# A two-layer transformer block on one core: a written-out loop on the PE, reordered ACT and DVE pieces, and a third weight buffer

## The chip, the core and the metric

The kernel runs on one core of one Trainium2 chip. The metric is device time in microseconds (us), lower is better. The core has five engines that run their own instruction streams and meet only at semaphores: PE (TensorE, the matrix multiplier), DVE (VectorE), ACT (ScalarE), POOL (GpSimd) and SP, which here only issues DMAs.

## The reference

The program computes two layers (`DEPTH = 2`) over 512 latent tokens and 256 context tokens of width 1024, in fp32.

```python
for l in range(DEPTH):
    need_ctx = l < DEPTH - 1
    a_lat = modulate(x, norm1_g[l], mod_lat[0], mod_lat[1])      # rms_norm(x, g) * (1 + scale) + shift
    a_ctx = modulate(h, norm1_g[l], mod_ctx[0], mod_ctx[1])
    m_lat, m_ctx = token_mixers(a_lat, a_ctx, w_in[l], w_out[l], ...)   # attention | retention | Fourier
    x = x + mod_lat[2] * m_lat
    x = x + mod_lat[5] * sq_relu_mlp(modulate(x, norm2_g[l], mod_lat[3], mod_lat[4]), w_ff1[l], w_ff2[l])
    if need_ctx:
        h = h + mod_ctx[2] * m_ctx
        h = h + mod_ctx[5] * sq_relu_mlp(modulate(h, ...), w_ff1[l], w_ff2[l])
```

`sq_relu_mlp(h, w1, w2)` is `square(relu(h @ w1)) @ w2` with a hidden width of 4096. The retention part needs tables of decay factors, made with exp from `ret_decay_logit[l]`. Context tokens are carried through the first layer only; the second layer updates the latent tokens alone.

## The kernel before

**Layout.** The residual stream `X` stands transposed: 8 tiles (m = 0 to 7) of 128 features by 768 tokens, the 512 latent ones first. Every fp32 product is made of three matmuls with operands split in a high and a low part: high by high, high by low, low by high. So every weight tile goes through three hands: SP loads 128x1024 values to `raw` (`w_load`, line 339), ACT copies them to `Whi` (`hi`, line 658, one at line 663), POOL subtracts to get `Wlo` (`low_parts`, line 521). `raw`, `Whi` and `Wlo` have two slots; unit u of the weights uses slot u % 2, and a slot comes free when the PE has finished the unit two before. At the end of the first layer there is a third slot (`raw3`, which lies in `macc`, and `W3`), used in turn with the other two by 13 units (`in_tail`, `slot_of`, `slot_before`, `raw_count`, lines 280 to 298).

**Order.** Everything is ordered by hand: each engine's function (`_(sp)`, `_(pool)`, `_(act)`, `_(dve)`, `_(pe)`) lists its work in program order, and a wait at the head of an engine's stream holds all behind it. Loop variable l is 0 for the first layer and 1 for the second. Per layer: 18 units of the input projection (`for u in range(UP)`, five groups g of output columns), transposes, retention and attention, 8 units of the output projection, then the MLP: four tiles of the first weight matrix, seven `half(c, ...)` of four tiles of the first and four units of the second matrix each, and a rest.

**The PE's loops.** In the first layer `half(0)`, `half(1)` and `half(2)` are written out on the PE and `half(3)` to `half(6)` are a hardware loop of two passes of two halves (line 2056). In the second layer three passes of two halves are a loop (line 2099). In the first layer the halves also turn modulation sums (`mod_sums`, four transposes from `macc`, line 1577) after their fifth and eighth unit.

**The norms.** `NORMS` numbers six of them: 1 and 2 are the ones ahead of the first layer's MLP (latent, context), 3 and 4 those at the start of the second layer (latent, context), 5 the one ahead of the second layer's MLP. A norm n goes through these pieces: ACT squares each of the 8 tiles of `X` as soon as its residual is added (`stat_squares`, line 688, alternately to `sqb[:, 0]` and `sqb[:, 1]`), DVE adds the squares up to `sq_sums` (`sq_add`, line 1118), the PE sums over features with matmuls against ones (`stats`, line 1595: first `sq_sums`, which holds tiles 0 to 6, then tile 7), ACT takes the root (`norm_root`), DVE the reciprocal, the PE spreads it (`spread`), and then for every tile DVE multiplies (`norm_full`, line 1092), ACT makes the high part (`norm_hi`, line 706) and DVE (even tiles; all tiles in norms 3 and 4) or POOL (odd tiles) the low part.

**The second layer's start.** In the input projection's first group (units 0 to 3) four banks of PSUM fill; ACT copies them to `Pq` after unit 3 (line 814), and unit 4 overwrites them. Beside that ACT makes the decay tables: `prep` (line 722, after unit 1) and `prep_tables` (line 733, after unit 2), 17 instructions in all with three loads of function tables; DVE makes `prep_gains`, `prep_masks` and the squares of the queries (`q_squares`) by the list `work` (line 1289).

## Time and profile before

| | before |
|---|---|
| median of 3 runs | 1704.47 us (1702.3 to 1705.03) |
| the profiled execution | 1702.21 us |
| its span, first to last instruction | 1700.4 us |
| mean granted PE clock | 0.977 |
| PE busy | 1606.9 us, 94% |
| DVE busy | 1042.7 us, 61% |
| ACT busy | 588.5 us, 35% |
| POOL busy | 584.6 us, 34% |

The busy shares are averages over stages. The span is 1.8 us shorter than the execution's own time, which also holds what lies before the first and behind the last instruction. Positions in the text ("at 813.95") are us from the span's start. A matmul is listed with the length of its pipeline, so neighbours overlap; the distance between two starts is what one costs. Two records of the same kind may stand merged in one row, with their number behind x.

### The profile page before, as it was taken

How to read it: one execution, taken by the hardware profiler on the slowest of the kernel's cores; microseconds unless marked ns; L12 is line 12 of the kernel's file. 1: busy time of each engine (PE TensorE's matmuls, PEld its weight loads, DVE VectorE, ACT ScalarE, POOL GpSimd, SP SyncE). 2: the span in 40 equal slices, each digit the busy share in tenths (PEclk: the TensorE clock that was granted, in tenths of full speed). 3: DMA queues.
4: the chain of work that ended last, by engine and by line, in shares of the span. 5: the costliest groups of instructions: out<-in, count | busy, mean ns of one | idle time of the engine just before them, and what ended most of it. 6: DMA issues, size and time to landing. Idle time of an engine off the chain costs nothing.

```text
span 1700.4 us, 23038 instructions
## 1 busy us (share of the span) xinstructions
PE 1606.9 (94%) x8800; PEld 1365.0 (80%) x8800; DVE 1042.7 (61%) x1481; ACT 588.5 (35%) x951; POOL 584.6 (34%) x324
## 2 busy tenths in 40 slices
PE   6899989989999999999899988998999799999998
PEld 2788878978888888888788887887897688888887
DVE  5778966868765767566466776585544544444442
ACT  4522435652532221211212345234662432332321
POOL 1336661012333222233222443336003444444442
PEclk9899999989999999999999999999999899999999
DMA  9333111105333434344343432231002132333332
GB/s 325 101 126 118 51 44 50 51 9 154 94 99 116 120 112 131 99 142 133 91 143 103 129 110 75 71 91 38 1 1 82 55 99 88 97 95 90 99 99 87
DMA packets 168653, 162.33 MB, mean 95 GB/s; under 512 B 6624, under 2 KB 132208, under 8 KB 168560
## 3 DMA queue, kind: packets, MB, share of 16 engines
q1 hardware_dynamic: 168560, 161.02, 31.1%
q8 instruction: 67, 1.10, 0.3%
q14 instruction: 26, 0.21, 0.0%
HBM read 158.90 MB, written 2.10 MB: 95 GB/s over the span
## 4 chain that ended last, share of the span: by engine, by line
PE 57%; issue 25%; DVE 7%; POOL 4%; ACT 4%; DMA 1%; SPq 1%; POOLq 0%; DVEq 0%; ACTq 0%
PE psA L1931 17%; PE psB L1931 16%; POOL Wlo L525 4%; PE psA L1711 2%; PE psA L1712 2%; PE psA L1713 2%; PE psB L1711 2%; PE psB L1713 2%; PE psB L1712 2%; PE ps L1903 2%; DVE Ab L1438 1%; PE psS L1713 1%; PE psS L1712 1%; PE psS L1711 1%; PE psS L1572 1%
## 5 line engine op out<-in xcount | busy, mean ns | idle before, releaser
L525 POOL TENSOR_TENSOR Wlo<-raw,Whi 128x1024 fp32r<-128x1024 f32 x158 | 384.5, 2434 | 829.8 <-ACT Whi L663 829.8
L663 ACT ACTIVATE Whi<-raw 128x1024 fp32r<-128x1024 f32 x181 | 191.4, 1059 | 635.0 <-PE psB L1931 269.4
L1438 DVE TENSOR_TENSOR Ab<-Tb 128x512 f32<-128x512 f32 (+2 forms) x68 | 167.9, 2469 | 175.9 <-ACT Tb L929 175.8
L1931 PE MATMUL psA<-Ahi,Whi 128*128 128x512 f32 (+1 forms) x432 | 138.1, 362 | 11.4 <-issue 5.0
L1931 PE MATMUL psB<-Ahi,Whi 128*128 128x512 f32 (+1 forms) x424 | 135.1, 362 | 2.6 <-POOL Wlo L529 2.2
L1931 PE MATMUL psA<-Ahi,Wlo 128*128 128x512 f32 (+1 forms) x432 | 137.5, 361 | 0.0
L1931 PE MATMUL psA<-Alo,Whi 128*128 128x512 f32 (+1 forms) x432 | 136.8, 359 | 0.0
L1931 PE MATMUL psB<-Ahi,Wlo 128*128 128x512 f32 (+1 forms) x424 | 134.9, 361 | 0.0
L1211 DVE SCALAR_TENSOR_TENSOR X<-psB,modT,X 128x256 f32<-128x256 f32 (+1 forms) x104 | 67.1, 664 | 109.7 <-PE psB L1931 109.6
L1931 PE MATMUL psB<-Alo,Whi 128*128 128x512 f32 (+1 forms) x424 | 134.3, 359 | 0.0
L1931 PE MATMUL psA<-Hhi,Whi 128*128 128x512 f32 (+1 forms) x368 | 117.7, 362 | 14.1 <-DVE X L1211 12.8
L1211 DVE SCALAR_TENSOR_TENSOR X<-psA,modT,X 128x256 f32<-128x256 f32 (+1 forms) x104 | 67.0, 662 | 86.2 <-PE psA L1931 86.1
L1039 DVE SCALAR_TENSOR_TENSOR macc<-modraw,csil,macc 128x512 f32<-128x512 f32 x126 | 113.2, 957 | 10.4 <-DMA modraw<-in_w_mod_dram 10.4
L1931 PE MATMUL psA<-Hhi,Wlo 128*128 128x512 f32 (+1 forms) x368 | 116.6, 359 | 0.0
L1931 PE MATMUL psB<-Hhi,Wlo 128*128 128x512 f32 (+1 forms) x368 | 116.3, 358 | 0.0
L1931 PE MATMUL psA<-Hlo,Whi 128*128 128x512 f32 (+1 forms) x368 | 115.9, 357 | 0.0
L1931 PE MATMUL psB<-Hhi,Whi 128*128 128x512 f32 (+1 forms) x368 | 115.9, 357 | 0.0
L1931 PE MATMUL psB<-Hlo,Whi 128*128 128x512 f32 (+1 forms) x368 | 115.7, 357 | 0.0
L931 ACT ACTIVATE Hhi<-Ab 128x512 fp32r<-128x512 f32 (+2 forms) x68 | 48.2, 708 | 176.6 <-DVE Ab L1438 176.6
L1931 PEld LDWEIGHTS psA<-Ahi,Whi 128*128 128x128 f32 x432 | 74.5, 190 | 25.0 <-issue 7.9
L1931 PEld LDWEIGHTS psA<-Hhi,Whi 128*128 128x128 f32 x368 | 62.8, 189 | 29.0 <-issue 9.8
L1440 DVE TENSOR_TENSOR Hlo<-Ab,Hhi 128x512 fp32r<-128x512 f32 (+2 forms) x68 | 53.5, 786 | 52.7 <-ACT Hhi L931 52.7
(331 smaller groups left out, 3525.9 us busy)
## 6 DMA issues: line engine op xcount, KB each, us to landing
raw<-in_w_ff_dram SPq DMA_DIRECT2D x135, 512.0 KB, 4.1
modraw<-in_w_mod_dram SPq DMA_DIRECT2D x72, 512.0 KB, 4.3
raw<-in_w_in_dram SPq DMA_DIRECT2D x36, 512.0 KB, 3.7
modst<-in_w_mod_dram SPq DMA_DIRECT2D x16, 512.0 KB, 5.8
raw<-in_w_out_dram SPq DMA_DIRECT2D x16, 512.0 KB, 4.3
modat<-in_w_mod_dram SPq DMA_DIRECT2D x8, 512.0 KB, 3.8
macc<-in_w_ff_dram SPq DMA_DIRECT2D x5, 512.0 KB, 3.5
modraw<-in_dft_lat_dram SPq DMA_DIRECT2D x8, 257.0 KB, 3.6
```

The source lines that it names most:

```text
L525: nc.gpsimd.tensor_tensor(Wlo[:, s, :], raw[:, s, :], Whi[:, s, :], ALU.subtract).then_inc(S["lo_done"], 1)
L663: nc.scalar.activation(whis[slot], raws[slot], ACT.Copy).then_inc(S["hi_done"], 1)
L931: nc.scalar.activation(Hhi[:, hpar, k, c0:c1], Ab[:, k % 2, c0:c1], ACT.Copy).then_inc(S["h_hi"], 1)
L1039: ins = V.scalar_tensor_tensor(out=acc[:, s, :], in0=src[:, kk * MCH:(kk + 1) * MCH], scalar=col, in1=acc[:, s, :], op0=ALU.mult, op1=ALU.add)
L1211: last = V.scalar_tensor_tensor(out=X[:, m, c0:c1], in0=pair[p][:, c0:c1], scalar=modT[:, l, 8 * chunk + m, s:s + 1], in1=X[:, m, c0:c1], ...
L1438: V.tensor_tensor(Ab[:, k % 2, c0:c1], Tb[:, k % 2, c0:c1], Tb[:, k % 2, c0:c1], ALU.mult).then_inc(S["h_full"], 1)
L1440: V.tensor_tensor(Hlo[:, hpar, k, c0:c1], Ab[:, k % 2, c0:c1], Hhi[:, hpar, k, c0:c1], ALU.subtract).then_inc(S["h_lo"], 1)
L1711: mm(out, ah, wh, start=first, stop=False)
L1712: mm(out, ah, wl, start=False, stop=False)
L1713: last = mm(out, al, wh, start=False, stop=fin)
L1903: last = mm((ps6, ps7)[b % 2][:, h * HD:(h + 1) * HD], PTs[:, it % 2, i * P:(i + 1) * P], Pk[:, kt, P + (h // 4) * HD:P + (h // 4 + 1) * H ...
L1931: last = mm(dst[:, c0:c1], wt, x[:, i, c0:c1], start=f, stop=e)
```

## The change

- **The PE's loop in the first layer is written out.** `half(3)` to `half(6)` become four straight copies.
- **Token sums in three parts.** DVE adds only tiles 0 to 5 to `sq_sums`; the PE sums `sq_sums`, then tile 6 from `sqb[:, 0]`, then tile 7 from `sqb[:, 1]`. The last `sq_add` of each of the norms 1 to 5 goes, and each `stats` gets one more round of token-tile matmuls (4 for latent, 2 for context tokens).
- **Norm pieces behind residuals.** In norm 3 DVE and ACT take the context residuals 4 to 7 ahead of the last norm tiles: DVE's order becomes residuals 2, 3, tiles 3, 4, residuals 4, 5, tile 5, residuals 6, 7, tiles 6, 7. Before norm 1's root ACT no longer squares the first context tile.
- **Decay tables in units 4 and 5** (counted from 0) of the second layer's projection on ACT, after the group's copies to `Pq`, instead of units 1 and 2. DVE's list follows: query squares in unit 3, gains in 4, masks in 6.
- **A third slot for one weight** (`THIRD`, the third tile of the second layer's MLP): it goes to slot 2, so it is loaded and split before the first two tiles have been used; ACT splits it right behind norm 5's root and POOL subtracts it ahead of norm 5's tiles. ACT's split of the second tile moves behind the squares of norm 5.

```diff
@@ -277,25 +277,31 @@
+    THIRD = BASE[1] + UP + UO + 2
+
     def in_tail(u):
...
-        return (2, 1, 0)[(u - TAIL0) % 3] if in_tail(u) else u % 2
+        return 2 if u == THIRD else (2, 1, 0)[(u - TAIL0) % 3] if in_tail(u) else u % 2
...
             return u - 3
-        return u - (4 if u == BASE[1] + 1 else 2)
+        if u == THIRD:
+            return BASE[1] - 1
+        return u - (4 if u in (BASE[1] + 1, THIRD + 2) else 2)
...
             return (u - TAIL0) // 3 + 1 + ((TAIL0 + 1) // 2, TAIL0 // 2, 0)[slot_of(u)]
-        return u // 2 + 1 - ((2, 3)[u % 2] if u >= BASE[1] else 0)
+        if u == THIRD:
+            return (BASE[1] - 1 - TAIL0) // 3 + 2
+        return u // 2 + 1 - ((3 if u > THIRD else 2, 3)[u % 2] if u >= BASE[1] else 0)
@@ -480,7 +486,8 @@
             for k in range(4):
-                w_load(uf + k, (uf + k) % 2, r8((uf + k) % 2), ff1_src(l, k), False)
+                slot = slot_of(uf + k)
+                w_load(uf + k, slot, raws[slot].rearrange("p (k n) -> p k n", k=8), ff1_src(l, k), False)
                 if l == 0 and k:
@@ -649,8 +656,11 @@
                 low_parts(uf - UO + 2, uf + 2)
+                pool.wait_ge(S["hi_done"], THIRD + 1)
+                nc.gpsimd.tensor_tensor(wlos[2], raws[2], whis[2], ALU.subtract).then_inc(S["lo_done"], 1)
                 norm(5)
-                low_parts(uf + 2, UNITS)
+                low_part(uf + 3)
+                low_parts(uf + 4, UNITS)
@@ -667,6 +677,8 @@
                     sem, value = "mod_used", MOD1 + 48 - MOD0
+                if u == THIRD:
+                    sem, value = "lin_ready", LIN[1] + 1
                 hi(slot_of(u), raw_count(u) - 1, sem, value)
@@ -690,7 +702,7 @@
             if m >= 2:
-                act.wait_ge(S["sq_sum"], 6 * n - 6 + (1 if m == 2 else m - 2))
+                act.wait_ge(S["sq_sum"], 5 * n - 5 + (1 if m == 2 else m - 2))
             if m == KT - 1 and c0 == 0:
@@ -820,9 +832,9 @@
                         norm_hi(4, k)
-                if u == 1:
+                if u == (1, 4)[l]:
                     prep(l)
-                if u == 2:
+                if u == (2, 5)[l]:
                     prep_tables(l)
@@ -939,8 +951,8 @@
                 hi_static(uf)
+                norm_root(1)
                 stat_squares(2, 0, S["resid_done"], 9)
-                norm_root(1)
                 hi_static(uf + 1)
@@ -955,18 +967,25 @@
                 for u in range(UO):
-                    hi_static(u0 + UP + u + 2)
+                    if u < 7:
+                        hi_static(u0 + UP + u + 2)
                     if u >= 1:
...
                 stat_squares(5, 7, S["resid_done"], RES[1] + 8)
-                norm(5)
+                hi_static(uf + 1)
+                norm_root(5)
+                hi_static(THIRD)
+                for k in range(KT):
+                    norm_hi(5, k)
             for k in range(4):
-                if l or k:
+                if l == 0 and k or k == 3:
                     hi_static(uf + k + 2)
+                elif l and k < 2:
+                    hi_static(uf + k + 3)
                 relu(hid + k, 0, k % 2, k, lin + k + 1, first, LAT if l == 0 and k >= 2 else 0)
-            past = ((0, 0), (2, 3))[l]
+            past = ((0, 0), (3, 3))[l]
@@ -993,7 +1012,7 @@
                 norm_root(3)
-                for his, ms, ks in (((0, 1), (0, 1), (0, 1)), ((2,), (), (2,)), ((3,), (2, 3), (3, 4)), ((4,), (), (5, 6)), ((5,), (4, 5), (7,)), ((6, 7), (6, 7), ())):
+                for his, ms, ks in (((0, 1), (0, 1), (0, 1)), ((2,), (), (2,)), ((3,), (2, 3), (3, 4)), ((4,), (), ()), ((5,), (4, 5), (5,)), ((6, 7), (6, 7), (6, 7))):
                     for i in his:
@@ -1120,7 +1139,7 @@
             if m > 1:
-                dve.wait_ge(S["sq_sum"], 6 * n - 6 + m - 1)
+                dve.wait_ge(S["sq_sum"], 5 * n - 5 + m - 1)
             V.tensor_tensor(sq_sums[:, c0:c1], sqb[:, 0, c0:c1] if m == 1 else sq_sums[:, c0:c1], sqb[:, m % 2, c0:c1], ALU.add).then_inc(S["sq_sum"], 1)
@@ -1288,7 +1307,7 @@
             else:
-                work = {2: [(prep_gains, l)], 5: [(prep_masks, l)], 6: [(q_squares, t) for t in range(NT)], 8: [(k_squares,)],
+                work = {3: [(q_squares, t) for t in range(NT)], 4: [(prep_gains, l)], 6: [(prep_masks, l)], 8: [(k_squares,)],
                         9: [(qk_roots,)] + [(rq, t) for t in range(NL)] + [(qk, 0), (qk, 1)],
@@ -1443,7 +1462,7 @@
                     resid(0, 2, m, m % 2, m + 1, LATENT)
-                    if m >= 2:
+                    if 2 <= m < KT - 1:
                         sq_add(1, m - 1)
...
@@ -1537,17 +1556,17 @@
                     resid(0, 5, m, m % 2, end + 4 + m + 1, LATENT)
-                    if m >= 2:
+                    if 2 <= m < KT - 1:
                         sq_add(3, m - 1)
...
                     resid(0, 5, m, m % 2, end + 12 + 3 * (m // 2) + m % 2 + 2, CONTEXT)
-                    if m >= 2:
+                    if 2 <= m < KT - 1:
                         sq_add(4, m - 1)
-                for ms, js in (((0, 1), (0, 1, 2)), ((2, 3), (3, 4, 5, 6)), ((4, 5), (7,)), ((6, 7), ())):
+                for ms, js in (((0, 1), (0, 1, 2)), ((2, 3), (3, 4)), ((4, 5), (5,)), ((6, 7), (6, 7))):
                     for m in ms:
@@ -1594,8 +1613,10 @@
-            pe.wait_ge(S["sq_sum"], 6 * n)
+            pe.wait_ge(S["sq_sum"], 5 * n)
             token_sums(n, sq_sums, True, False)
+            pe.wait_ge(S["stat_sq"], 8 * n - 1)
+            token_sums(n, sqb[:, 0], False, False)
             pe.wait_ge(S["stat_sq"], 8 * n)
@@ -2053,9 +2074,8 @@
                 half(2, 0, 2)
-                with pe.Fori(0, 2) as cc:
-                    half(cc * 2 + 3, 1, 1)
-                    half(cc * 2 + 4, 0, 1)
+                for c in range(3, 7):
+                    half(c, c % 2, 1)
                 for k in range(4):
```

**Place 1: the PE, from half(4) to half(5) of the first layer.** `ps<-ident,macc` are the last transposes of half(4), `psA<-Ahi,Whi` the first matmuls of the next half. Before:

```order
L1931 MATMUL psB<-Hhi,Wlo 128x256
L2044 REGISTER_ALU
L1577 ISA [waits mod_used,mod_evac]
L1572 MATMUL ps<-ident,macc 128x128 [waits mod_step]
L1572 MATMUL ps<-ident,macc 128x128 x3
L2056 REGISTER_ALU
L2056 COMPARE_AND_BRANCH
L1931 MATMUL psA<-Ahi,Whi 128x256 [waits resid_done,lo_done]
L1931 MATMUL psA<-Alo,Whi 128x256
L1931 MATMUL psA<-Ahi,Wlo 128x256
```

and with the change:

```order
L1952 MATMUL psB<-Hhi,Wlo 128x256
L1591 MATMUL ps<-ident,macc 128x128 [waits mod_step,mod_used,mod_evac]
L1591 MATMUL ps<-ident,macc 128x128 x3
L1952 MATMUL psA<-Ahi,Whi 128x256 [waits resid_done,lo_done]
L1952 MATMUL psA<-Alo,Whi 128x256
L1952 MATMUL psA<-Ahi,Wlo 128x256
L1952 MATMUL psA<-Ahi,Whi 128x256
```

The counter and the branch back to the loop's head are gone; the next half stands in the stream right behind the transposes.

**Place 2: ACT, units 2 to 5 of the second layer's input projection.** `Whi<-raw` is the split of a weight unit, `lgt` and `decay` belong to the tables, `Pq<-psA` and `Pq<-psB` are the copies that free the first group's banks. Before:

```order
L713 ACTIVATE Ahi<-Ab,modT 128x256 [waits a_full] x2
L725 ACT_TABLE_LOAD
L725 ACTIVATE lgt<-lgt 128x8 [waits prep_lg]
L726 ACT_TABLE_LOAD
L726 ACTIVATE lgt<-lgt 128x8 [waits act]
L663 ACTIVATE Whi<-raw 128x1024 [waits unit_done,raw_in0]
L740 ACT_TABLE_LOAD [waits tmp_in]
L740 ACTIVATE decay<-tmpt,lgt 128x128 [waits prep_lg]
L740 ACTIVATE decay<-tmpt,lgt 128x128 x3
L741 ACTIVATE ZE<-lgt,tmpt 128x4
L743 ACTIVATE XQ<-tmpt,lgp 128x128 x2
L740 ACTIVATE decay<-tmpt,lgt 128x128 x4
```

and with the change:

```order
L673 ACTIVATE Whi<-raw 128x1024 [waits unit_done,raw_in0]
L826 ACTIVATE Pq<-psA 128x2x4x64 [waits proj_ready] x2
L826 ACTIVATE Pq<-psB 128x2x4x64 [waits proj_ready]
L826 ACTIVATE Pq<-psB 128x2x4x64 [waits unit_done]
L673 ACTIVATE Whi<-raw 128x1024 [waits unit_done,raw_in1]
L673 ACTIVATE Whi<-raw 128x1024 [waits unit_done,raw_in0]
L737 ACT_TABLE_LOAD
L737 ACTIVATE lgt<-lgt 128x8 [waits prep_lg]
L738 ACT_TABLE_LOAD
L738 ACTIVATE lgt<-lgt 128x8 [waits act]
L673 ACTIVATE Whi<-raw 128x1024 [waits unit_done,raw_in1]
L752 ACT_TABLE_LOAD [waits tmp_in]
```

The copies to `Pq` now come ahead of both parts of the tables, and two more splits do as well.

**Place 3: ACT, end of the second layer's output projection and norm 5.** `sqb<-X` are the squares, `warm` is a one-column root that has the function table loaded, `rstd<-psS` is the norm's root. Before:

```order
L696 ACTIVATE sqb<-X 128x512 [waits sq_sum,resid_done]
L663 ACTIVATE Whi<-raw 128x1024 [waits lin_ready,raw_in1]
L696 ACTIVATE sqb<-X 128x512 [waits sq_sum,resid_done]
L695 ACT_TABLE_LOAD [waits sq_sum]
L695 ACTIVATE warm<-epst 128x1 [waits resid_done]
L696 ACTIVATE sqb<-X 128x512 [waits act]
L703 ACTIVATE rstd<-psS,epst 128x4 [waits stat_done]
L713 ACTIVATE Ahi<-Tb,modT 128x512 [waits a_full] x2
L713 ACTIVATE Tb<-Tb,modT 128x512
L713 ACTIVATE Ahi<-Ab,modT 128x512 [waits a_full] x2
```

and with the change:

```order
L708 ACTIVATE sqb<-X 128x512 [waits sq_sum,resid_done] x2
L707 ACT_TABLE_LOAD [waits sq_sum]
L707 ACTIVATE warm<-epst 128x1 [waits resid_done]
L708 ACTIVATE sqb<-X 128x512 [waits act]
L673 ACTIVATE Whi<-raw 128x1024 [waits lin_ready,raw_in1]
L715 ACTIVATE rstd<-psS,epst 128x4 [waits stat_done]
L673 ACTIVATE W<-macc 128x1024 [waits lin_ready,raw_in2]
L725 ACTIVATE Ahi<-Tb,modT 128x512 [waits a_full] x2
```

The split in front of the seventh square is now behind the eighth, and the split of the third tile (`W<-macc`) stands between the root and the first norm tile.

## Rows read from the trace of the kernel before

**Rows 1.** waits of the PE: for whom, us in total, times, longest

```profile
PE psA L1931 <- DVE X L1211: 13.1, 13, 3.2
...
PE psA L1931 <- issue: 5.0, 1, 5.0
```

**Rows 2.** timeline of the PE, 808 to 815: start, us, what, [idle before]

```profile
808.33 0.60 PE L1572 MATMUL ps<-ident,macc 128*128 128x128 f32 x4
813.95 0.80 PE L1931 MATMUL psA<-Ahi,Whi 128*128 128x512 f32 x2 [5.03 <-issue]
```

**Rows 3.** busy by stretch: PE, PEld, DVE, ACT, POOL, clock, DMA, GB/s

```profile
813.95:824.24 10.29, 10.29 (x49) 8.86 (x48) 0.00 (x0) 0.00 (x0) 0.00 (x0) 0.80 0.36 104
824.24:832.72 8.48, 8.48 (x51) 7.36 (x49) 4.93 (x4) 2.61 (x3) 2.40 (x1) 1.00 0.00 0
...
1052.00:1057.00 5.00, 5.00 (x12) 3.95 (x13) 4.86 (x5) 2.22 (x4) 2.36 (x1) 0.50 0.00 0
1329.00:1333.50 4.50, 4.50 (x11) 3.53 (x12) 4.24 (x7) 3.89 (x7) 2.57 (x2) 0.51 0.02 4
```

**Rows 4.** queue 8 in 741:771, then in 803:823: packets, MB, share

```profile
q8 instruction: 1, 0.02, 0.3%
...
q8 instruction: 3, 0.05, 0.9%
```

**Rows 5.** timeline of the PE, 1445 to 1446

```profile
1445.39 0.39 PE L1931 MATMUL psA<-Ahi,Whi 128*128 128x512 f32 x1
```

**Rows 6.** timelines of ACT, then of the PE, 1045 to 1052

```profile
1045.98 1.28 ACT L740 ACT_TABLE_LOAD   x1
...
1051.26 1.05 ACT L814 ACTIVATE Pq<-psA 128x512 f32<-128x512 f32 x2
...
1046.81 0.39 PE L1713 MATMUL psB<-Whi,Alo 128*128 128x512 f32 x1
1051.98 0.77 PE L1711 MATMUL psA<-Whi,Ahi 128*128 128x512 f32 x1 [4.78 <-ACT Pq L814]
```

**Rows 7.** the token sums of norm 1 (line 1592): busy PE, PEld

```profile
425.60:427.40 1.80, 1.73 (x16) 1.80 (x16) 1.00 0.00 0
```

**Rows 8.** timelines of DVE, ACT and the PE, 1317 to 1329

```profile
1318.78 2.42 DVE L1124 TENSOR_TENSOR Ab<-Ab,sqb 128x512 f32<-128x512 f32 x1 [0.92 <-ACT sqb L696]
...
1318.77 1.28 ACT L695 ACT_TABLE_LOAD   x1
...
1320.30 0.63 ACT L696 ACTIVATE sqb<-X 128x512 f32<-128x512 f32 x1
...
1321.25 1.86 PE L1592 MATMUL psS<-ones,Ab 128*128 128x1 f32 x8 [4.18 <-DVE Ab L1124]
...
1328.98 0.76 PE L1931 MATMUL psA<-Ahi,Whi 128*128 128x512 f32 x1 [2.48 <-DVE Alo L1089]
```

**Rows 9.** timelines of ACT, then of the PE, 1341 to 1346

```profile
1341.65 1.06 ACT L663 ACTIVATE Whi<-raw 128x1024 fp32r<-128x1024 f32 x1 [5.53 <-PE psA L1931]
1342.61 0.58 ACT L929 ACTIVATE Tb<-psA 128x512 f32<-128x512 f32 x1
...
1345.17 0.50 PE L1931 MATMUL psA<-Ahi,Whi 128*128 128x512 f32 x1 [2.95 <-POOL Wlo L525]
```

**Rows 10.** timelines of POOL, then of DVE, 1031 to 1035

```profile
1031.88 2.39 POOL L525 TENSOR_TENSOR Wlo<-raw,Whi 128x1024 fp32r<-128x1024 f32 x1 [5.46 <-ACT Whi L663]
...
1032.24 2.32 DVE L1089 SCALAR_TENSOR_TENSOR Alo<-Tb,modT,Ahi 128x256 fp32r<-128x256 f32 x1 [0.46 <-ACT Ahi L713]
```

**Rows 11.** timelines of POOL, then of the PE, 1011 to 1024

```profile
1011.98 2.42 POOL L649 TENSOR_TENSOR Wlo<-raw,Whi 128x1024 fp32r<-128x1024 f32 x1 [5.01 <-ACT Whi L663]
...
1021.50 4.92 POOL L649 TENSOR_TENSOR Wlo<-raw,Whi 128x1024 fp32r<-128x1024 f32 x2 [4.33 <-ACT Whi L663]
...
1015.49 0.35 PE L1931 MATMUL psA<-Hhi,Whi 128*128 128x256 f32 x1 [3.21 <-DVE X L1211]
...
1023.99 0.47 PE L1711 MATMUL psA<-Whi,Ahi 128*128 128x512 f32 x1 [0.85 <-issue]
```

4 lines of the change are left out of this document (2 added, 2 removed).

## The prediction

> **What bounds the kernel.** I read the share of busy time first: the PE is busy for 94% of the span, the next engine for 61%. So the end is set by the PE, and an edit is worth what it takes from the PE's idle time, from its work, or from its time at the half clock. Then the PE's waits, longest first. The largest total is for DVE's residuals [rows 1], but that is 13 short waits at the heads of half chunks, and the change does not touch most of them. The second row is one single wait of 5.0 us put down to "issue": the PE waited for nothing that another engine does. Third, the timelines around the PE's long waits, to see what ended each, and the busy time by stretch, whose clock column tells where matmuls ran at half speed (0.50 is 1.2 GHz, 1.00 is 2.4 GHz). The change touches five places.
>
> **A. The loop written out.** The issue wait stands at 813.95, behind the transposes that end half(4) [rows 2]: it is the branch back, between the loop's two passes. The tile behind it took 10.29 us at a mean clock of 0.80, the same tile next 8.48 at 1.00 [rows 3], so the idle time also cost 10.29 - 8.48 = 1.8 us at the half clock. Together 5.0 + 1.8 = 6.8 us. Is it code? In 20 us around it queue 8, which carries instructions, moved 3 packets; in 30 us around the end of half(3), inside the pass, it moved 1 [rows 4], and the PE had no wait there. So straight code is brought in ahead of the PE and the jump back is not. What comes due next when the wait goes: the weights' low part (POOL) and the residual, both done well before 813.95, since the wait is put down to neither. I take -6.8. Bounds: 0, if the wait is not the branch's, and -6.8.
>
> The Trainium skill speaks against this ("Advanced Engine Details and Errata", ISA Cache): the TensorE's instruction cache holds 128 KB in lines of 16 KB, 256 instructions each. A pass has by the code 784 matmuls (two halves of 384, and 16 transposes) and as many weight loads, which by the page is about 100 KB and would stay in the cache; then the 5.0 us are not a fetch and may stay. The trace does not agree, for it shows the 3 packets. By the page's rule A would be 0.
>
> The second layer's loop, with half the matmuls in a pass, goes back at 1445.39 without a wait [rows 5]; it stays a loop and I give it nothing.
>
> **B. Decay tables behind the copies.** Unit 4 of the second layer's projection waits 4.78 us for ACT's copy of `Pq` [rows 6]. ACT's row shows why: its table load begins at 1045.98 and the exps behind it end just before the copies start at 1051.26, 5.3 us, while the PE's last matmul of the group started at 1046.81. The new order has the copies first. Three of the four banks are complete while the PE still works on the last one, so unit 4, which starts on the first bank, should not wait at all: -4.8. Behind the wait the PE ran at 0.50 from 1052 to 1057 [rows 3]: 5.0 x (1 - 0.5) = 2.5 us lost, which goes with the wait: -2.4 (a little kept for a remaining handover). What is moved must find room: `prep` takes 3 loads and small exps, `prep_tables` the 5.3 us. A unit of the second group lasts about 7 us on the PE and ACT has only a 1 us split in each, so each part fits in front of the next split. Their consumers are far off (DVE's masks, the retention). B = -7.2; bounds -4.8 (clock lost anyway) and -7.3.
>
> **C. Norm 5.** Before: DVE's last add of squares ran from 1318.78 to 1321.20, and the PE's sums started at 1321.25 after 4.18 us idle [rows 8], so the output projection ended at 1317.07. Now the PE needs tiles 0 to 5, added long before, then tile 6, squared one split earlier, then tile 7. ACT's function table loads from 1318.77 to 1320.05, and the last square starts at 1320.30. In the new order the load waits only for an add of squares, so it falls before the residual. The residual is in at 1317.86 (DVE's 0.92 idle before 1318.78), so the last square ends at about 1317.9 + 0.25 + 0.63 = 1318.8. The PE sums 12 token tiles at 1.73/8 = 0.22 each [rows 7], 2.6 us from 1317.07: end 1319.7, with no wait. Before, the sums ended at 1321.25 + 2 x 1.8 = 1324.85, and the first matmul of the MLP came 4.1 later. That distance gives 1323.8.
>
> But the third weight's low part is now in the way. ACT splits the second tile at 1318.8 to 1319.8, POOL subtracts it to 1322.2, then the third tile to 1324.6, 2.4 us each as in [rows 10]. Those rows show what that does to DVE: a low part of a norm tile which started 0.36 us after POOL's subtraction took 2.32 us and ended 0.29 after it. So the first low part of norm 5 ends near 1324.9, and the MLP starts at 1325.1 instead of 1328.98: -3.9. The half clock at the MLP's start (4.5 us in [rows 3], 2.2 lost) I leave as it is, since idle time of 2 to 3 us remains in front. The Trainium skill ("SBUF — State Buffer", SBUF: two separate sides) says the same, that DVE operations with two SBUF inputs and POOL lock each other out for a whole instruction; without that rule the start would be 1323.8 and the sum 1.3 lower. Bounds of C: 0, if POOL delays more than that, and -3.9 - 1.3 - 2.2 = -7.4.
>
> **The third slot.** The third tile waits 2.95 us for POOL [rows 9]. Its weights are now ready, but it writes the bank of the first tile, so it needs that tile's relu. ACT does the split of the fourth tile first (it waits for the second tile's end, the pair's end) and then the relu: 1.06 + 0.58 + 0.1 = 1.7 us. So the wait shrinks to 1.7: -1.2. Bounds 0 and -2.9.
>
> **D. Norm 3 beside the context's MLP.** The PE waits 3.21 us for residual 4 until 1015.49 [rows 11], because DVE has norm tiles 5 and 6 in front. Now residuals 4 and 5 come first, and the next bar is the weight's low part, 1011.98 + 2.42 = 1014.40: 1.1 us earlier. The second tile's residual does not hold it either, some 0.9 more. The second layer starts at 1023.99 when the low part of its first unit is done, which hangs on the end of these tiles (POOL starts at 1021.50), so it moves with them. I take -2.0; bounds 0 and -3.2.
>
> **E. More token tiles.** Norms 1 to 4 add 4 + 2 + 4 + 2 = 12 at 0.22 us on the PE: +2.6, all on the path, since no wait of the PE stands in front of those sums. DVE's saved adds are worth nothing there. The moved root of norm 1 costs nothing: the squares behind it are needed some 15 us later.
>
> Sum: -6.8 - 7.2 - 3.9 - 1.2 - 2.0 + 2.6 = -18.5. Against the profiled execution's own 1702.21 that is 1683.7. The median of the runs shown is 2.3 higher (1704.47), which would give 1686.0; I take the middle, 1685.
>
> **Rivals.**
> 1. *The branch is not what costs.* A gives 0 and the rest -11.7: 1702.2 - 11.7 and half of the 2.3 = 1691.7. For it: the page above, and a loop in the same program that costs nothing. Against: the packets. 0.08.
> 2. *POOL's queue delays norm 5.* If the third tile's weights come late or its split holds ACT, POOL's odd low parts wait behind it and C and the third slot give 0: -13.4, 1690.0. For it: POOL now has two subtractions in a row, 4.8 us, in front of the norm. Against: SP may issue the third load as soon as the one before it is out, 5 us earlier. 0.12.
> 3. *Clock and locks fall better.* If the half clock ahead of the MLP goes too (C = -6.1) and D gives -3.2: -21.9, 1681.5. 0.1.
> 4. *Slower: straight code is fetched in the open.* One place, the 135 us of half(3) to half(6) that now run through new code: by the 1 packet in 20 to 30 us of [rows 4] some 5 to 7 more packets. At the price of the branch, 6.8 us each, 6 packets cost 41, less the 18.5 is +22.5: about 1726. It decides from 3.1 us a packet on (18.5/6). Against it: the first pass of the loop was fetched the same way with no wait. 0.02.
>
> **Chances.** Forecast (1682 to 1688.5) 0.68, rivals 0.08, 0.12, 0.10, 0.02. The range 1678.5 to 1692.5 takes in the first three rivals and the bounds of each term. What a measurement here tells from no change is about 0.2%, 3.4 us. Faster by more: 0.96; within: 0.02; slower: 0.02.
>
> **What would show it.** A: no issue wait in the first layer's MLP, one packet of queue 8 in 20 to 30 us throughout, and no stretch at half clock near 808. B: unit 4 starts right behind unit 3, ACT's loads 10 us after it, clock 1.00. C: sums of norm 5 right behind the output projection, the first low part of norm 5 long (near 2 us) beside POOL. Third slot: a wait of about 1.7 for `Tb` instead of `Wlo`. D: the wait before residual 4 named POOL, about 2 us. E: 12 token tiles in each latent norm. It is wrong if new waits in the written-out halves appear, or if the PE's wait ahead of unit 4 only changes its name.

## The result, and the profile after

| | before | after |
|---|---|---|
| median | 1703.51 us (4 runs, 1702.3 to 1705.03) | 1683.09 us (4 runs, 1682.13 to 1685.04) |
| ratio | | 0.988, 95% interval 0.9864 to 0.9895 |
| the profiled execution, its span | 1702.21, 1700.4 us | 1682.13, 1680.3 us |
| mean granted PE clock | 0.977 | 0.985 |

The change made the kernel 20 us faster; 1685.0 was predicted, with a range of 1678.5 to 1692.5. Later, on another chip and in other rounds, the same kernel gave 1686.68 against 1702.41, ratio 0.9898 (0.9882 to 0.9915).

To see where the 20.1 us of span went I cut both traces at the same instructions of the PE. First the kernel after, then the kernel before (the timeline of the PE; start, us, what, [idle before]):

```profile
406.53 0.41 PE L1591 MATMUL ps<-ident,macc 128*128 128x128 f32 x2 [1.65 <-DVE macc L1058]
508.66 0.40 PE L1952 MATMUL psA<-Hhi,Whi 128*128 128x512 f32 x1
951.43 0.44 PE L1635 MATMUL ps<-tmpt 128*128 128x64 f32 x3
1016.51 0.47 PE L1732 MATMUL psA<-Whi,Ahi 128*128 128x512 f32 x1 [1.75 <-issue]
1134.17 0.33 PE L1591 MATMUL psB<-ident,Pq 128*128 128x128 f32 x1 [0.47 <-ACT Pu L826]
1310.07 0.76 PE L1952 MATMUL psA<-Ahi,Whi 128*128 128x512 f32 x1 [3.20 <-DVE Alo L1108]
1357.83 0.39 PE L1952 MATMUL psA<-Hhi,Whi 128*128 128x512 f32 x1
```

```profile
408.10 0.30 PE L1572 MATMUL ps<-ident,macc 128*128 128x128 f32 x1 [1.77 <-DVE macc L1039]
507.56 0.40 PE L1931 MATMUL psA<-Hhi,Whi 128*128 128x512 f32 x1
958.30 0.45 PE L1614 MATMUL ps<-tmpt 128*128 128x64 f32 x3
1148.56 0.33 PE L1572 MATMUL psB<-ident,Pq 128*128 128x128 f32 x1 [0.47 <-ACT Pu L814]
1377.95 0.39 PE L1931 MATMUL psA<-Hhi,Whi 128*128 128x512 f32 x1
```

The first instruction is a modulation transpose in the first layer's output projection; the second opens its MLP's second projection; the third is in the MLP's tail; then the first matmul of the second layer [rows 11], the first transposes behind its projection, the start of its MLP [rows 8], and the same point of that MLP as the second instruction is of the first. Distances between neighbours, in us, for all profiled runs but e4 (one execution each; the experiments are told below):

| | c: to 508.66 | d: to 951.43 | e: to 1016.51 | f: to 1134.17 | g: to 1310.07 | h: to 1357.83 |
|---|---|---|---|---|---|---|
| before | 99.46 | 450.74 | 65.69 | 124.57 | 180.42 | 48.97 |
| after | 102.13 | 442.77 | 65.08 | 117.66 | 175.90 | 47.76 |
| after, other chip | 102.24 | 446.31 | 64.97 | 117.64 | 175.95 | 47.71 |
| e1 loop back | 102.19 | 442.83 | 64.82 | 117.66 | 175.93 | 47.74 |
| e2 tables early | 103.70 | 442.14 | 66.23 | 124.28 | 176.54 | 47.79 |
| e3 two-part sums | 99.52 | 446.33 | 63.59 | 117.21 | 176.84 | 48.07 |
| e5 before, shifted | 99.48 | 442.18 | 66.26 | 125.14 | 180.74 | 49.05 |
| e6 loop, two-part | 99.51 | 452.08 | 64.20 | 117.77 | 176.56 | 47.91 |
| e7 third slot, norm 3 undone | 100.58 | 445.36 | 67.21 | 117.64 | 175.72 | 52.60 |
| e8 two moves | 102.09 | 446.30 | 64.15 | 119.19 | 177.07 | 46.57 |
| e10 norm 5 in two | 102.15 | 446.31 | 65.79 | 117.62 | 177.02 | 48.34 |
| e11 three moves | 102.15 | 444.22 | 64.15 | 119.23 | 175.82 | 45.36 |
| e12 moves, two-part | 99.49 | 444.19 | 62.27 | 117.77 | 175.53 | 46.66 |

Before minus after: c +2.7, d -8.0, e -0.6, f -6.9, g -4.5, h -1.2; what lies in front of 408.10 gave -1.6; behind h (322.5 in both) nothing. The sum is -20.1. Of g's -4.5, 3.85 lie at norm 5 (below); the other 0.7 lie ahead of it, where the runs differ by up to 1.1 us and I found no cause.

The rows behind the first columns, all of the kernel after. The PE's waits (for whom, us in total, times, longest), which answer [rows 1], with the issue wait of the loop gone:

```profile
PE psA L1952 <- DVE X L1230: 9.9, 11, 1.5
...
PE psA L1952 <- ACT Tb L941: 1.8, 1, 1.8
PE psA L1732 <- issue: 1.7, 1, 1.7
```

The timeline of the PE where [rows 2] had the wait (the transposes now start at 808.45), then the busy time by stretch (columns as in [rows 3]) for the tile at that place, for unit 4's first 5 us, and for the start of the second MLP:

```profile
808.80 0.59 PE L1952 MATMUL psA<-Ahi,Whi 128*128 128x512 f32 x2
```

```profile
808.80:817.37 8.57, 8.57 (x52) 7.45 (x51) 4.40 (x6) 0.91 (x1) 2.39 (x1) 1.00 0.44 126
1046.90:1052.00 5.10, 5.10 (x25) 4.22 (x24) 4.25 (x10) 4.05 (x5) 2.48 (x1) 1.00 0.12 38
1310.07:1314.50 4.43, 4.43 (x11) 3.46 (x12) 4.16 (x7) 3.67 (x6) 2.29 (x2) 0.50 0.50 137
```

No wait and clock 1.00 where [rows 3] had 0.80 and 0.50; only the MLP's start still runs at 0.50 (1.2 GHz). Unit 4 starts at 1046.90 right behind unit 3 (its last matmul at 1046.78), and ACT's loads of the two decay pieces come at 1048.24 and 1055.14.

### The profile page after: what moved, and what is told of

Same layout as the page of the kernel before. It is cut to its first block, busy times and chain, and to the rows that moved or that the text cites. A ratio compares the mean times of both kernels' runs of the same rounds, so it can differ in the third digit from the quotient of the medians.

```text
span 1680.3 us, 23001 instructions
## 1 busy us (share of the span) xinstructions
PE 1602.7 (95%) x8832; PEld 1364.8 (81%) x8832; DVE 1038.6 (62%) x1476; ACT 588.7 (35%) x951; POOL 583.7 (35%) x324
## 4 chain that ended last, share of the span: by engine, by line
PE 75%; DVE 9%; issue 8%; ACT 4%; DMA 2%; POOL 1%; SPq 0%; DVEq 0%; ACTq 0%; POOLq 0%
PE psA L1952 26%; PE psB L1952 26%; PE psA L1732 2%; PE psB L1732 2%; PE psA L1733 2%; PE psA L1734 2%; PE psB L1733 2%; PE psB L1734 2%; PE ps L1924 2%; DVE Ab L1457 2%; DVE macc L1058 2%; PE psS L1734 1%; PE psS L1733 1%; PE psS L1732 1%; PE ps L1591 1%
## 5 line engine op out<-in xcount | busy, mean ns | idle before, releaser
L532 POOL TENSOR_TENSOR Wlo<-raw,Whi 128x1024 fp32r<-128x1024 f32 x156 | 379.3, 2432 | 811.4 <-ACT Whi L673 811.4
L1952 PE MATMUL psA<-Ahi,Whi 128*128 128x512 f32 (+1 forms) x424 | 134.2, 359 | 4.2 <-DVE Alo L1108 3.2
L1952 PE MATMUL psA<-Ahi,Wlo 128*128 128x512 f32 (+1 forms) x424 | 133.6, 358 | 0.0
L1952 PE MATMUL psA<-Alo,Whi 128*128 128x512 f32 (+1 forms) x424 | 133.0, 356 | 0.0
```

Of the source, the lines that this page charges most:

```text
L532: nc.gpsimd.tensor_tensor(Wlo[:, s, :], raw[:, s, :], Whi[:, s, :], ALU.subtract).then_inc(S["lo_done"], 1)
L1952: last = mm(dst[:, c0:c1], wt, x[:, i, c0:c1], start=f, stop=e)
```

## The experiments

### A: is it the loop?

**e1**, the loop put back in the kernel after:

```diff
-                for c in range(3, 7):
-                    half(c, c % 2, 1)
+                with pe.Fori(0, 2) as cc:
+                    half(cc * 2 + 3, 1, 1)
+                    half(cc * 2 + 4, 0, 1)
```

> The changed kernel with one edit undone: the PE's halves 3 to 6 of the first layer are again a loop of two passes. Theory (the jump back is what cost): an issue wait of about 5.0 us stands again behind half 4, the tile behind it takes about 10.3 us instead of 8.57 at a mean clock near 0.80, and the time is 6.8 us above the changed kernel's: about 1690 against 1683.1. Rival (the gain came from how the rest of the program lies, not from the jump): no issue wait, time within 1 us of 1683.

Measured: ratio to before 0.9897 (0.9881 to 0.9913), as the kernel after. The wait did not return, and stretch d is 442.83 against 442.77. The first matmul behind the jump, in the timeline of the PE, follows 0.36 us behind the start of half(4)'s transposes:

```profile
811.41 0.59 PE L1952 MATMUL psA<-Ahi,Whi 128*128 128x512 f32 x2
```

My theory, that the jump back is what costs, fell. The reason showed in the instruction queue: in 125 us of the loop's second pass (820:945) no packet of queue 8 is left in e1, in the kernel before there are 6. DMA by queue in that stretch, e1 and then before (packets, MB, share):

```profile
q1 hardware_dynamic: 14816, 14.57, 39.4%
```

```profile
q1 hardware_dynamic: 14021, 14.17, 38.8%
q8 instruction: 6, 0.10, 0.3%
```

So in e1 the second pass ran from code that was still there, and in the kernel before it was fetched again. Both passes have the same 1,629 instructions (matmuls, weight loads, waits). What differs is where they lie: the built program has the loop at instruction 7391 in the kernel before and at 7415 in e1, because the third part of the sums in norms 1 and 2 adds 6 token tiles, 24 instructions. Two runs put that to the test from both sides.

**e5**, the kernel before with nothing but 24 PE instructions more at its start, in a wait:

```diff
         tr(ps7[:, 96:144], rows[0:48, 1, :], 48).then_inc(S["rows_T"], 1)
+        for i in range(6):
+            mm(psS[:, 0:1], ident[:, :], ident[:, 0:1], start=True, stop=True)
```

> The kernel before with nothing but 6 matmuls of one column more at its start, on the PE, where it waits for its first weights (results unused). They are 24 instructions of the PE with their weight loads, so the loop of the first layer begins at instruction 7415 of the PE's program instead of 7391, as in the changed kernel with its loop put back, which showed no wait at the jump. Theory (the 5 us are a fetch that happens or not by where the loop lies, its 1,629 instructions touching one 256-instruction block more or less): no issue wait behind half 4, no instruction packets during the second pass, and 6 to 7 us less than before: ratio 0.996. Rival (the wait went for another reason, such as the changed order of the other engines): the wait of 5.0 us stays, ratio 1.000.

Measured: 1694.4 against 1700.75 us, ratio 0.9964 (0.9948 to 0.9981). The wait is gone, with the loop in place (transposes at 806.48):

```profile
806.84 0.59 PE L1933 MATMUL psA<-Ahi,Whi 128*128 128x512 f32 x2
```

**e6**, the kernel after with the loop of e1 and the sums of norms 1 to 4 in two parts (the diff of e3 below), which puts the loop at 7391 again:

> The changed kernel with the loop put back and the token sums of norms 1 to 4 in two parts: 24 PE instructions fewer in front of the loop, which so begins at instruction 7391 again, as in the kernel before. Theory (place of the loop): the issue wait of about 5.0 us is back behind half 4, with a burst of 3 instruction packets in 10 us around it and about one every 20 us through the second pass. Rival (something else that the change moved): no issue wait, no packets in the second pass, as with the loop put back alone.

Measured: 1689.14 us in one run, and the wait is back, and longer. Timeline of the PE, then the stretch behind it (clock 0.83), then queue 8 in 803:823:

```profile
813.04 0.80 PE L1954 MATMUL psA<-Ahi,Whi 128*128 128x512 f32 x2 [6.23 <-issue]
```

```profile
813.04:823.50 10.46, 10.46 (x51) 8.99 (x51) 0.00 (x0) 0.19 (x1) 0.00 (x0) 0.83 0.29 92
```

```profile
q8 instruction: 3, 0.05, 1.0%
```

Four programs, two places, two outcomes. The packets of queue 8 over the whole run say the same: 58 in e1 and e5, 67 in before and e6, though all four have 14,908 to 14,972 PE instructions. The kernel after, 16,517 instructions, has 64. With 58 packets for some 14,950 instructions a packet is about 258 of them, so the 9 packets more are about the whole pass of 1,629 (6.3 packets' worth), if one counts what is cut at its ends and what is brought in ahead.

The Trainium skill ("Advanced Engine Details and Errata", ISA Cache) gives 128 KB and lines of 256 instructions. By it 1,629 instructions are 6.4 lines and touch 7 or 8, depending on where they start, of the 8 that fit. If one line is brought in ahead, which I assume, 8 touched would be one too many. The runs agree in the line's size (258 by the packets) and in the two outcomes. They don't show the boundary itself: counted from the program's first instruction both places touch 8 lines (7391 is 223 into its line, 7415 is 247), so the account also needs 9 to 32 further instructions in front of them, which nothing here shows. That the place of the loop decides is shown; that it does so by this count of lines is not.

**e4** looked at the same thing before I knew this, in the second layer's loop:

```diff
                         ff2(c, par, k - 4, uu, slot, span)
+                    if l and not isinstance(c, int):
+                        for i in range(25):
+                            mm(psS[:, 0:1], ident[:, :], ones[:, :], start=True, stop=True)
```

> The changed kernel with 200 matmuls of one column added to every pass of the second layer's loop (25 behind each tile of the second projection, results unused), so that a pass of it has 584 matmuls instead of 384; the first layer's loop in the kernel before had 784. Theory (a jump back costs where the pass is longer than some size between 384 and 784 matmuls): an issue wait of 1 to 7 us appears at each of the two jumps back, near the end of the second and of the fourth half. Rival (what cost was particular to the first layer's loop): no issue wait at the jumps. The time itself is higher by the added matmuls in either case, 3 x 200 x about 0.11 = 66 us.

The expectation miscounted its own edit. The added matmuls stand behind all 8 tiles of a half, and each of them is two matmuls on the PE, so a pass has 1,184 matmuls instead of 584, 2,417 instructions with loads and waits, and the time is 2127.91 us, 445 more (2,400 matmuls at 0.186 us, the clock at 0.7 to 0.8). What it shows: queue 8 has 94 packets for 18,117 PE instructions, some 24 more than 258 to a packet would make, and at the first jump back there are 3 of them in 12 us, the burst that before and e6 have. So this longer pass does not stay. But the PE hardly waits for it: nothing at the first jump, and at the second

```profile
1809.57 0.79 PE L1952 MATMUL psA<-Ahi,Whi 128*128 128x512 f32 x1 [0.43 <-issue]
```

Why the same burst costs 5.0 and 6.2 us in the first layer's loop and at most 0.4 here stays open; neither theory had that.

### B: the decay tables

**e2** puts both pieces back in front of the copies:

```diff
-                if u == (1, 4)[l]:
+                if u == 1:
                     prep(l)
-                if u == (2, 5)[l]:
+                if u == 2:
                     prep_tables(l)
```

(DVE's list of work for these units likewise.)

> The changed kernel with the decay tables of the second layer back in units 1 and 2 (ACT and DVE as in the kernel before). Theory: unit 4 waits about 4.8 us for ACT's copies of Pq again and the PE runs at half clock for about 5 us behind it; the time is 7.2 us above the changed kernel's, about 1690.3. Rival: the tables' wait was already covered by something else that the change moved, so that 0 to 4.8 us come back and the clock does not fall: 1683 to 1688.

Measured: ratio 0.993 (0.9912 to 0.9947), 0.3 to 0.5% above the kernel after's two ratios (its interval is clear of the first and meets the second, so the trace decides). Stretch f is 124.28 instead of 117.66, the 6.6 us, with the wait to the hundredth as in [rows 6] and less than full clock behind it:

```profile
1051.09 0.47 PE L1732 MATMUL psA<-Whi,Ahi 128*128 128x512 f32 x1 [4.78 <-ACT Pq L826]
```

```profile
1051.09:1056.09 5.00, 5.00 (x15) 4.00 (x16) 4.86 (x5) 2.25 (x4) 2.37 (x1) 0.66 0.00 0
```

### C and the third slot: norm 5

In the kernel after, timelines of ACT, POOL, DVE and the PE, the answer to [rows 8, 9]:

```profile
1300.84 1.28 ACT L707 ACT_TABLE_LOAD   x1 [2.07 <-DVE Ab L1143]
1303.07 0.63 ACT L708 ACTIVATE sqb<-X 128x512 f32<-128x512 f32 x1
...
1307.03 2.35 POOL L660 TENSOR_TENSOR W<-macc,W 128x1024 fp32r<-128x1024 f32 x1
...
1308.45 1.48 DVE L1108 SCALAR_TENSOR_TENSOR Alo<-Tb,modT,Ahi 128x512 fp32r<-128x512 f32 x1
...
1301.86 0.39 PE L1611 MATMUL psS<-ones,Ab 128*128 128x1 f32 x3
1310.07 0.76 PE L1952 MATMUL psA<-Ahi,Whi 128*128 128x512 f32 x1 [3.20 <-DVE Alo L1108]
1325.09 0.47 PE L1952 MATMUL psA<-Ahi,W 128*128 128x512 f32 x1 [1.78 <-ACT Tb L941]
```

The sums start right behind the output projection, the table load is over before the last residual, and the MLP starts 8.21 us after the sums' start. To compare with before, one point is needed for both: the start of the projection's last matmul, 1301.63 after and 1316.69 before. From it the MLP's start is 8.44 us away after and 12.29 before. That is -3.85. The third slot's POOL subtraction (1307.03 to 1309.38) holds DVE's first low part, 1.48 us.

**e10**, the sums of norm 5 alone in two parts (`ADDS` counts DVE's adds by norm):

```diff
+    ADDS = (0, 5, 5, 5, 5, 6)
-            pe.wait_ge(S["sq_sum"], 5 * n)
+            pe.wait_ge(S["sq_sum"], sum(ADDS[:n + 1]))
             token_sums(n, sq_sums, True, False)
-            pe.wait_ge(S["stat_sq"], 8 * n - 1)
-            token_sums(n, sqb[:, 0], False, False)
+            if ADDS[n] == 5:
+                pe.wait_ge(S["stat_sq"], 8 * n - 1)
+                token_sums(n, sqb[:, 0], False, False)
```

> The changed kernel with the token sums of norm 5 alone in two parts again. Theory of the prediction (the sums waited for DVE's last add of squares, 2.42 us beside POOL): the wait of about 4 us in front of the sums returns and the MLP of the second layer starts about 12 us after the output projection's end instead of 8.2. Rival (most of the gain came from ACT's function table, loaded before the last residual now, and from POOL's low part, which no longer stands beside the add): the add takes 0.68 us and ends near 1.5 us behind the output projection, the sums are 16 instead of 24, and the MLP starts within 0.5 us of where it does in the changed kernel.

Measured: 1689.66 us in one run, with stretch d alone 3.5 us longer than in the kernel after. DVE's last add and the PE:

```profile
1309.73 0.68 DVE L1144 TENSOR_TENSOR Ab<-Ab,sqb 128x512 f32<-128x512 f32 x1
...
1310.46 0.38 PE L1612 MATMUL psS<-ones,Ab 128*128 128x1 f32 x2 [1.45 <-DVE Ab L1144]
1317.08 0.76 PE L1954 MATMUL psA<-Ahi,Whi 128*128 128x512 f32 x1 [2.99 <-DVE Alo L1109]
```

The add takes 0.68 us, not the 2.42 of [rows 8], since the split that feeds POOL's next subtraction now stands behind the last square. The sums wait 1.45, are 8 token tiles instead of 12, and the MLP starts 8.45 us after the start of the projection's last matmul (1308.63): the same as with three parts. So the three parts bring nothing in norm 5 as the rest stands, and the new order is enough for the 3.85 us. Two things in it are not told apart: the load ahead of the residual and the add without POOL beside it. Nor was it run what three parts give with the order of before.

**e7** undoes the third slot (its slot, POOL's and ACT's order) and, far from it, the order of norm 3:

```diff
-for his, ms, ks in (..., ((3,), (2, 3), (3, 4)), ((4,), (), ()), ((5,), (4, 5), (5,)), ((6, 7), (6, 7), (6, 7))):
+for his, ms, ks in (..., ((3,), (2, 3), (3, 4)), ((4,), (), (5, 6)), ((5,), (4, 5), (7,)), ((6, 7), (6, 7), ())):
-                hi_static(THIRD)
```

> The changed kernel with two edits undone at places far from each other: the third slot for the one MLP weight, and the order of norm 3 beside the context's MLP. Third slot, theory: the third tile of the second layer's MLP waits near 2.95 us for POOL instead of 1.79 for ACT's Tb, while DVE's first low part of norm 5 falls from 1.48 to 0.75 us, since POOL no longer subtracts beside it, so the first tile starts 0.7 us sooner: the third slot's net is 0.4 us. Rival: the low part stays at 1.4 or more and the third slot is worth its whole 1.2. Norm 3, theory: the wait before residual 4 is named DVE again, near 3.2 us, with matmuls at half clock behind it; the stretch from the third tile of the latents' last products to the second layer's first matmul (49.66 us in the changed kernel) grows by 1 to 2 us. Rival: it grows by no more than 0.3, since the order only changed the name of the wait. In all 1 to 3 us above the changed kernel: about 1685.

Measured: 1690.52 us in one run. The third slot first, DVE's low part, the third tile's wait, and the tile behind it:

```profile
1312.76 0.75 DVE L1096 SCALAR_TENSOR_TENSOR Alo<-Tb,modT,Ahi 128x512 fp32r<-128x512 f32 x1
...
1330.60 0.79 PE L1940 MATMUL psA<-Ahi,Whi 128*128 128x512 f32 x1 [2.95 <-POOL Wlo L528]
```

```profile
1330.60:1339.05 8.45, 8.45 (x25) 6.69 (x25) 4.37 (x4) 2.69 (x4) 2.38 (x1) 0.63 0.46 124
```

Both halves of the theory came: without POOL beside it the low part is 0.75, and the first tile starts 7.1 us after the sums' start (1306.55) instead of 8.21; in return the third tile waits 2.95 instead of 1.78. The net would be nothing, were it not for the clock: this time the tile behind the wait ran at 0.63 and took 8.45 us instead of 5.54, which the same wait in the kernel before did not bring about, and the two tiles ahead of it took 0.8 more. So the expected 1685 was missed by 5.5, most of it clock (3.7). Norm 3: stretch e is 67.21 instead of 65.08, the 2.1 us, and the wait before residual 4 was 4.03 us, for DVE. Of the 2.1, 1.1 are the longer wait and the rest mostly the clock behind it, less a shorter wait for issue ahead of the second layer.

### D and what is late next

The kernel after, timelines of POOL and the PE, against [rows 11]:

```profile
1006.36 2.34 POOL L656 TENSOR_TENSOR Wlo<-raw,Whi 128x1024 fp32r<-128x1024 f32 x1 [4.05 <-ACT Whi L673]
...
1008.76 0.39 PE L1952 MATMUL psA<-Hhi,Whi 128*128 128x256 f32 x1 [2.92 <-POOL Wlo L656]
```

The wait is for POOL now, as predicted, but 2.92 us and not 2, because the matmuls in front of it have no waits of their own any more. Behind it the clock stayed at 1.00; in the kernel before it was 0.78 over the same 48 matmuls, which took 1.65 us longer. That part isn't the order's doing: e10 has the same order and a wait of 2.93 us, and there the clock fell, to 0.77 over the same 48 matmuls (1014.25:1021.77, 7.52 us instead of 6.00).

**e8** moves ACT's split for it ahead of two norm tiles, and the first relu of the second MLP ahead of a split:

```diff
-((3,), (2, 3), (3, 4)), ((4,), (), ())
+((3,), (2, 3), ()), ((4,), (), (3, 4))
-                elif l and k < 2:
+                elif l and k == 1:
                     hi_static(uf + k + 3)
                 relu(hid + k, 0, k % 2, k, lin + k + 1, first, LAT if l == 0 and k >= 2 else 0)
+                if l and k == 0:
+                    hi_static(uf + 3)
```

> The changed kernel with two further moves on ACT. First, in the context's MLP, the split of the tail's fifth weight stands in front of norm tiles 3 and 4 instead of behind them (it started at 1005.24 and POOL's low part, at 1006.36 to 1008.70, held the PE 2.92 us). Theory: it starts near 1001, POOL follows behind what it has in hand (until 1002.31), and the wait shrinks to 0.5 to 1.5 us. Rival: POOL's earlier subtraction stands beside DVE's low parts, which take 2.3 instead of 0.74 us, the residual comes late instead, and the wait only changes its name: 2 to 3 us. Second, in the second layer's MLP, the relu of the first tile stands before the split of the fourth weight. Theory: the third tile's wait of 1.78 us for Tb shrinks by the split's 0.96, to 0.8 or less. Rival: the fourth tile then waits for its low part as much. Together 2 to 3 us below the changed kernel: about 1680.

Measured: 1685.94 us in one run. The wait for `Tb` is gone (h 46.57, -1.2). The other wait is half as long, under another name, and the second layer starts behind 1.99 us of idle time at a lower clock:

```profile
1010.61 0.36 PE L1954 MATMUL psA<-Hhi,Whi 128*128 128x256 f32 x1 [1.45 <-DVE X L1232]
1018.76 0.47 PE L1734 MATMUL psA<-Whi,Ahi 128*128 128x512 f32 x1 [1.99 <-issue]
```

```profile
1018.76:1024.00 5.24, 5.24 (x21) 4.38 (x21) 4.33 (x7) 0.72 (x1) 2.70 (x1) 0.67 0.60 169
```

In the kernel after, behind 1.75 us of idle time, the same 5.24 us ran at 1.00. Stretch e gained 0.9 and f lost 1.5: on its own the move is worth nothing, and the run as a whole was not the 2 to 3 us faster that I expected. The rival was half right too: POOL's two subtractions (5.16 us from 1003.04) stood beside DVE, and one low part there took 2.23 us.

### E: more sums

**e3**, norms 1 to 4 in two parts (the diff of e10 with `ADDS = (0, 6, 6, 6, 6, 5)`):

> The changed kernel with the token sums of norms 1 to 4 in two parts again (12 token tiles fewer on the PE), norm 5 stays in three. Theory by the count alone: 12 x 0.22 = 2.6 us less, 1680.5. Rival, from the trace of the changed kernel: behind the 24 sums of norm 1 (2.6 us) the PE's clock is 0.62 in 426.69 to 431.14, and behind those of norm 3 it is 0.50 in 990.30 to 992.86, where the kernel before, with 16 sums (1.7 us), has 1.00; that adds 1.5 + 1.1 us, so 5.2 us less: about 1678. Third: DVE's fifth add of squares is late again and takes the place of the sums, no gain: 1683.

Measured: 1679.12 us, ratio 0.9871 (0.9854 to 0.9888). Stretch c falls by 2.6 (6 token tiles at 0.22 are 1.3), e by 1.5. Why twice the count: the stretches behind the sums of norms 1 and 3, first in the kernel after, then the same work before, when 8 token tiles and not 12 stood in front:

```profile
426.69:431.14 4.45, 4.45 (x26) 4.45 (x26) 0.55 (x2) 1.82 (x4) 2.38 (x1) 0.62 0.71 225
990.30:992.86 2.56, 2.56 (x14) 2.56 (x13) 0.48 (x1) 1.17 (x2) 2.56 (x2) 0.50 0.00 0
```

```profile
427.38:430.33 2.95, 2.95 (x26) 2.95 (x26) 0.55 (x2) 1.52 (x3) 1.49 (x1) 1.00 0.83 252
996.49:997.93 1.44, 1.44 (x14) 1.44 (x13) 0.48 (x1) 1.14 (x2) 1.44 (x1) 1.00 0.00 0
```

The same tiles cost 1.5 and 1.1 us more, at a clock of 0.62 and 0.50, behind 2.6 us of one-column matmuls; behind 1.7 us of them the clock stayed. The rival held in these two stretches. The total gained less than 5.2, since stretch d was 3.6 us longer, as it was in the kernel after's own other run (below).

All traces together bear this out for norm 3: the clock fell behind its sums in all nine with 24 matmuls there and in none of the five with 16. For norm 1 it fell in seven of the nine and in none of the five. The two exceptions are e1 and the other run of the kernel after. There it had fallen at the modulation transposes, 19 us ahead of the sums, and behind the sums it stayed (the other run, first at the transposes, then behind the sums):

```profile
408.47:412.00 3.53, 3.53 (x13) 3.15 (x14) 2.78 (x6) 0.63 (x1) 0.00 (x0) 0.52 0.69 190
430.25:433.20 2.95, 2.95 (x26) 2.95 (x26) 0.55 (x2) 1.82 (x4) 1.18 (x1) 1.00 1.01 325
```

Stretch c was as long as ever there, 102.19 and 102.24 us. In e6, with 16 matmuls, the clock fell at the transposes too, and c was 99.51. So in norm 1 the 24 matmuls don't always bring the fall, and why c is no shorter without it stays open.

### A version that beats both

**e9**, the kernel after again, beside **e11**, the moves of e8 and POOL's low part of the third slot's weight behind norm 5, and **e12**, these with the two-part sums of e3:

```diff
-                pool.wait_ge(S["hi_done"], THIRD + 1)
-                nc.gpsimd.tensor_tensor(wlos[2], raws[2], whis[2], ALU.subtract).then_inc(S["lo_done"], 1)
                 norm(5)
+                pool.wait_ge(S["hi_done"], THIRD + 1)
+                nc.gpsimd.tensor_tensor(wlos[2], raws[2], whis[2], ALU.subtract).then_inc(S["lo_done"], 1)
```

> The changed kernel itself, so that the two versions built on it are compared with it on the same chip and in the same rounds. Both theories expect the ratio measured before, 0.988.

> The changed kernel with three moves more: the two of the run before on ACT (the tail's fifth split in front of norm tiles 3 and 4, the first relu in front of the fourth split), and on POOL the low part of the third slot's weight behind norm 5 instead of in front of it. Theory from the traces: 1.1 us for the first (the stretch to the second layer was 48.53 instead of 49.66), 1.1 for the second (the wait for Tb was gone), and 0.7 for the third, since DVE's first low part of norm 5 takes 0.75 us instead of 1.48 without POOL beside it: 2.9 us less than the changed kernel, ratio to the kernel before near 0.9863. Rival: the waits only change their names and the time stays within 1 us of the changed kernel's, 0.988.

> The same three moves, and the token sums of norms 1 to 4 in two parts, those of norm 5 in three. Theory: 2.9 us for the moves and 4.5 for the sums (2.6 in norms 1 and 2, as in the run with two parts, 1.5 in norm 3 and 0.4 in norm 4): 7.4 less than the changed kernel, ratio near 0.9837. Rival: in the first layer's MLP the slower of the two matmul paces takes back 2 to 3 us, as it did in the run with two parts alone: ratio near 0.9853.

| | median, us | ratio to before | 95% interval |
|---|---|---|---|
| e9, after | 1686.68 | 0.9898 | 0.9882 to 0.9915 |
| e11 | 1681.86 | 0.9877 | 0.9860 to 0.9894 |
| e12 | 1677.85 | 0.9848 | 0.9831 to 0.9864 |

e12 is faster than the kernel after (the intervals don't meet), by 8.8 us; e11 lies between them and its interval meets both. In ratio each came out nearer its rival (0.988 and 0.9853) than its theory (0.9863 and 0.9837). The first low part of norm 5 and the MLP's start in e11, then the waits in the tail of e12:

```profile
1314.70 0.75 DVE L1110 SCALAR_TENSOR_TENSOR Alo<-Tb,modT,Ahi 128x512 fp32r<-128x512 f32 x1
...
1315.60 0.77 PE L1954 MATMUL psA<-Ahi,Whi 128*128 128x512 f32 x1 [2.47 <-DVE Alo L1110]
```

```profile
1005.98 0.36 PE L1956 MATMUL psA<-Hhi,Whi 128*128 128x256 f32 x1 [0.63 <-DVE X L1233]
1013.84 0.47 PE L1736 MATMUL psA<-Whi,Ahi 128*128 128x512 f32 x1 [0.85 <-issue]
```

1.48 us became 0.75, and the MLP's start moved from 8.21 us behind the sums' start to 7.1. The idle time ahead of the second layer was 2.00 us in e11 and the clock behind it 0.67, as in e8 (f is 119.23). The Trainium skill ("SBUF — State Buffer", SBUF: two separate sides) says that a DVE operation with two SBUF inputs and a POOL one exclude each other for a whole instruction; the traces agree: 0.75 us without POOL's subtraction beside it (e7, e11), 1.27 (e10), 1.48 (the kernel after) and 2.23 (e8) with it. In e12, with shorter sums, the idle time ahead of the second layer is 0.85 again, no clock is lost behind it (f is 117.77), and the move that was worth nothing in e8 shows in e: 62.27, against 63.59 in e3 and 64.20 in e6.

## Why the prediction was right, and where not

- **A, the loop, predicted -6.8.** The size came (the wait of 5.0 us and the clock behind it are gone; the other 1.2 of stretch d's -8.0 I put down to pace, below). The reason was wrong, so the right size was in part luck. The step that failed is "straight code is brought in ahead of the PE and the jump back is not": the jump costs nothing where no packet comes in its second pass (e1, e5), and the 24 instructions of the added sums in norms 1 and 2 alone take the wait away, with the loop kept. Writing out does so too: with the place of before, the loop waits (e6) and straight code doesn't (e3). I had set the page aside with "the trace does not agree, for it shows the 3 packets". The packets were right, and the page's sizes don't contradict them: I had compared bytes with bytes (100 KB in 128), where a count of the lines that the pass touches, with one ahead, leaves room for both outcomes. That count is an account that fits, and not shown. Rival 1 was right in its cause, that the written-out loop isn't what pays here, and wrong in its number.
- **B, the tables, predicted -7.2:** -6.9, and +6.6 when undone (e2).
- **C, norm 5, predicted -3.9:** -3.85. The step "now the PE needs tiles 0 to 5" was not what paid: with two parts the MLP starts just as early (e10). The new order did, the load ahead of the residual and the add without POOL beside it together. The lock on the first low part was there, 1.48 us long where near 2 was predicted.
- **Third slot, predicted -1.2:** the wait is 1.78 us, for `Tb` (predicted 1.7), and stretch h is 1.2 shorter. But the slot's subtraction also costs 1.1 at the MLP's start (e7), so its net, clock apart, was near nothing until POOL did it later (e11). The prediction had counted that price under C.
- **D, norm 3, predicted -2.0:** undone it costs 2.1 (e7). The wait itself hardly shrank, 3.21 to 2.92, and the clock behind it did not fall, 1.65 us for which the sum had no term and which was luck (e10).
- **E, the sums, predicted +2.6:** the mis-sized term. c +2.7 where 1.3 was due, and e was 1.5 and 0.9 lower without them (e3, e6) where 0.9 was due: some 4 us with norm 4's few tenths. The clock, which fell behind norm 3's 12 token tiles in every run that had them and behind norm 1's in most, had no term in the sum. "All on the path" did not hold for norm 3 either: 1.3 us of small waits ahead of residual 4 are gone with the longer sums (0.21 us in the kernel after and 0.23 in e7, 1.5 before and in e3).
- **No term at all:** -1.6 ahead of 408.10, -1.2 of pace in d and -0.7 in g ahead of norm 5. The first is no effect of the change that I can name: the instruction at 408.10 stood between 405.89 (e4) and 410.60 (e2) in these runs.

The errors were of both signs: E some 1.5 too cheap, start, pace and g 3.5 to the good. The total was nearer than its parts, and that was luck.
